# The last scan group of a Mamba-2 layer: ScalarE copies the gate units out of PSUM and applies the SiLU in place

## The reference

```
y = y + xs * d_skip
y = rmsnorm(y * silu(z), gnorm_w)
out = y @ w_out
```

## Time and profile before

| | |
|---|---|
| median of 3 runs | 1328.11 us (1326.69 to 1330.75) |
| the profiled execution, its own time | 1329.49 us |
| its span between first and last instruction | 1327.8 us |
| PE / DVE / ACT / POOL busy | 89% / 69% / 44% / 7% of the span |
| granted TensorE clock, mean | 0.949 of full |
| the last group, from its first x turn to the gated result | about 351 us to 432 us of the span |

### The profile page before, as it was taken

The page is one execution under the profiler, slowest core; times in us unless marked ns, Lnnn a source line. Parts: engine busy times, 40 slices in busy tenths (PEclk is TensorE's granted clock), DMA queues, the critical chain, the costliest instruction groups (busy, mean ns, idle before and its releaser), DMA issues.

```text
span 1327.8 us, 20149 instructions
## 1 busy us (share of the span) xinstructions
PE 1187.1 (89%) x7100; PEld 687.7 (52%) x7100; DVE 915.0 (69%) x1430; ACT 588.5 (44%) x1021; POOL 92.9 (7%) x106
## 2 busy tenths in 40 slices
PE   4999898998987689699999999997999968799997
PEld 2544464554544334244444444445845537688886
DVE  5696767758766889887888877637256656666554
ACT  4564654545545432233333432223334534566542
POOL 0004022050130000000000000000000000000000
PEclk9999898998999799799999999998999988899998
DMA  9331120111111446255645544430222102355552
GB/s 389 127 100 70 55 95 32 63 63 63 63 65 45 178 163 245 98 192 188 233 187 212 193 178 185 144 123 29 99 99 92 63 1 95 127 191 203 201 195 96
DMA packets 24526, 173.93 MB, mean 131 GB/s; under 512 B 2720, under 2 KB 2720, under 8 KB 5536
## 3 DMA queue, kind: packets, MB, share of 16 engines
q1 hardware_dynamic: 18432, 128.24, 26.2%
q0 software_dynamic: 5184, 37.75, 8.0%
q10 hardware_dynamic: 864, 7.34, 1.5%
HBM read 172.27 MB, written 1.05 MB: 131 GB/s over the span
## 4 chain that ended last, share of the span: by engine, by line
PE 73%; DVE 16%; issue 4%; ACT 4%; POOL 2%; DVEq 1%; DMA 0%; ACTq 0%; SPq 0%; POOLq 0%
PE bank L1482 19%; PE bank L1483 19%; PE bank L1484 19%; PE bank L1828 1%; DVE arena L995 1%; DVE arena L865 1%; PE bank L1686 1%; PE bank L1842 1%; PE bank L1675 1%; DVE arena L912 1%; PE bank L1509 1%; DVE wl L835 1%; DVE ssq L894 1%; DVE arena L907 1%; PE bank L1815 1%
## 5 line engine op out<-in xcount | busy, mean ns | idle before, releaser
L1482 PE MATMUL bank<-hh,wh 128*128 128x512 f16 (+1 forms) x1136 | 392.5, 346 | 20.6 <-DVE hl L903 7.7
L835 DVE SCALAR_TENSOR_TENSOR wl<-raw,wh 128x1024 f16<-128x1024 f32 x224 | 267.3, 1209 | 202.3 <-ACT wh L407 200.2
L1483 PE MATMUL bank<-hl,wh 128*128 128x512 f16 (+1 forms) x1136 | 391.8, 345 | 0.0
L1484 PE MATMUL bank<-hh,wl 128*128 128x512 f16 (+1 forms) x1136 | 391.4, 345 | 0.0
L407 ACT ACTIVATE wh<-raw 128x1024 f16<-128x1024 f32 x224 | 229.1, 1043 | 283.7 <-PE bank L1484 214.9
L1482 PE MATMUL bank<-arena,wh 128*128 128x512 f16 (+1 forms) x544 | 182.1, 335 | 11.1 <-DVE wl L835 3.7
L1483 PE MATMUL bank<-arena,wh 128*128 128x512 f16 (+1 forms) x544 | 182.0, 335 | 0.0
L1484 PE MATMUL bank<-arena,wl 128*128 128x512 f16 (+1 forms) x544 | 181.9, 334 | 0.0
L1482 PEld LDWEIGHTS bank<-hh,wh 128*128 128x128 f16 x1136 | 112.5, 99 | 123.9 <-issue 42.5
L865 DVE SCALAR_TENSOR_TENSOR arena<-arena,araw 128x1024 bf16<-128x1024 f32 x144 | 167.6, 1220 | 0.2
L1484 PEld LDWEIGHTS bank<-hh,wl 128*128 128x128 f16 x1136 | 112.4, 99 | 93.3 <-issue 5.7
(11 more groups left out here) (226 smaller groups left out, 1372.9 us busy)
## 6 DMA issues: line engine op xcount, KB each, us to landing
raw<-wgu SPq DMA_DIRECT2D x44, 1024.0 KB, 4.8
arena<-wadaT POOLq DMA_DIRECT2D x36, 1024.0 KB, 5.1
raw<-wdn SPq DMA_DIRECT2D x16, 896.0 KB, 4.5
raw<-wxg SPq DMA_DIRECT2D x12, 1024.0 KB, 4.9
arena<-wada SPq DMA_DIRECT2D x8, 1024.0 KB, 19.2
raw<-wz SPq DMA_DIRECT2D x8, 1024.0 KB, 4.8
raw<-wout SPq DMA_DIRECT2D x8, 1024.0 KB, 4.9
raw<-wdn SPq DMA_DIRECT2D x8, 1024.0 KB, 4.8
```

The lines of the kernel that those rows point to most:

```text
L835: ve.scalar_tensor_tensor(wl[:, u.slot, a:b], raw[:, u.slot, a:b], WS, wh[:, u.slot, a:b], ALU.mult, ALU.subtract).then_inc(lo_done, 1)
L1482: pe.matmul(o, wh[:, u.slot, wsl], ahi[:, k, t0:t1], start=st, stop=False)
L1483: pe.matmul(o, wh[:, u.slot, wsl], alo[:, k, t0:t1], start=False, stop=False)
L1484: i = pe.matmul(o, wl[:, u.slot, wsl], ahi[:, k, t0:t1], start=False, stop=en)
```

## The change

In the last group only, `z_raw` takes the place of `z_out`. It copies both banks into `zs` with Copy (counted by a new semaphore `zr_ok`) and then runs SiLU over `zs` in place, from SBUF to SBUF (counted by `zs_ok` as before). TensorE's waits ahead of units 1 and 2 go from `zs_ok` to `zr_ok`. The scale of 1/(WS*AS) moves to the copy.

```
+            def z_raw(k, u):
+                act.wait_ge(unit_done, u.half + (UD + 2))
+                for m in range(2):
+                    act.activation(zs[:, m, :], GB[m][:, :], ACT.Copy, scale=1.0 / (WS * AS)).then_inc(zr_ok, 1)
+                for m in range(2):
+                    act.wait_ge(zr_ok, 2 * k + m + 1)
+                    act.activation(zs[:, m, :], zs[:, m, :], ACT.Silu).then_inc(zs_ok, 1)
...
                 square_z(0)
-                z_out(u)
+                z_raw(0, u)
                 cvt(u.plus(2))
...
                 act.wait_ge(gl_ok, 2)
-                z_out(u.plus(1))
+                z_raw(1, u.plus(1))
                 square_z(2)
...
                 act.wait_ge(gl_ok, 4)
-                z_out(u.plus(2))
+                z_raw(2, u.plus(2))
...
+                    elif k == 0:
+                        pe.wait_ge(zs_ok, 2 * g + 1)
                     else:
-                        pe.wait_ge(zs_ok, 2 * g + 1 + 2 * k)
+                        pe.wait_ge(zr_ok, 2 * k)
```

More of the change, by code:

```diff
@@ L272, in build @@
         in_x = [sem("in_x0"), sem("in_x1")]
-        in_x_again, zp_ok = sem("in_x_again"), sem("zp_ok")
+        in_x_again, zp_ok, zr_ok = sem("in_x_again"), sem("zp_ok"), sem("zr_ok")
         in_ada = [sem(f"in_ada{i}") for i in range(ADA_FIRST)]
```

## The result

The changed kernel takes 1329.44 us (median of 20 runs, 1328.24 to 1330.80) against 1327.30 us for the kernel before (median of 20 runs, 1325.40 to 1330.75): 2.1 us more, a ratio of 1.0015 with a 95% interval of 1.0009 to 1.0022. It is slower, by less than the 0.3% named in the prediction.

What follows compares the result with a forecast made beforehand. ScalarE's path from unit 1's end to TensorE's `exponents` (3, 1) was taken as the bound. 0 (unit 0) + 1.2 (unit 1) + 0 (unit 2) + 1.7 (clock) = +2.9 us on 1328.11, so 1331.0 us; range 1327.3 to 1333.0.

Steps and rivals of the forecast that it cites:

- Unit 1, the first wait: TensorE's wait ahead of unit 2: copies without a table load let it start 1.29 us earlier.
- Unit 1, ScalarE's added time: ScalarE before `exps` (2, 3): two SBUF SiLUs at 0.52 each plus a 0.12 drain add 1.2 us.
- Where they meet: TensorE ahead of `exponents` (3, 1): the wait for `exps` (2, 3) grows from 1.30 to about 3.8 us, losing 1.2.
- Units 0 and 2: Last group's other two units: ScalarE's delay at unit 0 is covered, TensorE does not wait at unit 2; cost 0.
- the prediction's bound for unit 0: ScalarE at unit 0: if slower by 1.4 us, less 0.5 of cover, up to 0.9 us is lost.
- The clock: TensorE behind the 3.8 us pause: the clock falls to its lower level, costing 1.7 us (bounds 0 to 2.2).
- seven parts in ten: Chance given to TensorE losing its full clock behind the 3.8 us pause ahead of `exponents` (3, 1).
- The sum: Whole kernel: 0 for unit 0, 1.2 for unit 1, 0 for unit 2, 1.7 for the clock, +2.9 us.
- the rival in which the clock holds: TensorE behind the second pause keeps its clock; only ScalarE's 1.2 us is lost, 1329.3 us; chance 0.25.

Runs made afterwards that it cites:

- e4: Changed kernel with unit 1's two in-place SiLUs run twice: 1331.67 us against 1326.71 for the kernel before, ratio 1.0035.
- e5: Changed kernel with unit 1's SiLUs moved behind the group's last `exps` and VectorE's `gate(1)` moved later: 1325.25 us against 1328.75 for the kernel before.
- e2: Kernel before with the change at units 0 and 2 only, unit 1 keeping `z_out`: 1328.59 us against 1328.75 for the kernel before.
- a1: The changed kernel timed again, unaltered, on another chip: 1330.06 us against 1326.71 for the kernel before, ratio 1.0021.
- e1: Kernel before with the change at unit 1 only, units 0 and 2 keeping `z_out`: 1330.35 us against 1328.75 for the kernel before.
- e3: Changed kernel with TensorE writing step (3, 0)'s exponents eight times over, filling its second pause: 1329.69 us against 1328.75 for the kernel before.
- e6: The changed kernel with step (3, 0)'s exponents written eight times, timed again on another chip: 1328.67 us against 1326.71 for the kernel before.

## Why the prediction came out as it did

**Unit 1, the first wait.** Right: TensorE gained 1.43 us there (3.05 to 1.62), and none of it arrived at the end. The forecast was 1.29.

**Unit 1, ScalarE's added time.** Forecast 1.2 us, measured 1.05. The 0.12 for a drain ahead of the load is there, but I did not see that the copies, with no load ahead of them, begin 0.13 before `exps` has ended. The two cancel and leave the two SiLUs. The waits on `zr_ok` cost nothing that shows.

**Where they meet.** The second pause was forecast at 3.8 us and is 3.76. e4 lengthens ScalarE's list and the pause follows; e5 shortens it and the pause is gone. This shows that `exps` (2, 3), and not the emptying of the banks, sets this stretch.

**Units 0 and 2.** Costed at 0. e2 measures 0.01 us less on unit 0's ruler and 0.00 in the group. The slack was as thin as reckoned: `gate` waited 0.27 us for its SiLU. The Trainium skill (ScalarE: Activation LUTs, What ACT_TABLE_LOAD costs) adds a drain of 1.38 us to a table load. Here the trace does not agree: the copies end at 374.05, the load starts at 374.07 and ends at 375.35, and the SiLU starts at 375.36. No run here shows the drain. The 1.4 us in the prediction's bound for unit 0 stands in no row either; what the runs show there is `exps` (1, 0) 1.75 us late and nothing lost.

**The clock.** It fell, as forecast, in each of the four traces with this pause at 3.76 to 4.81 us (changed kernel, a1, e1, e4), and in neither of the two in which work filled it. The size was too small: 1.7 forecast, 2.14 measured on the path. I had reckoned `within` at its full-rate time and it too ran at half. So seven parts in ten looks too low for this pause, though all four traces are of longer executions (1330.45 to 1332.80 us) and none is from the lower heap. The sentence of the Trainium skill on idle gaps (TensorE: Matmul & The Clock Gate, Why this matters for your kernels; the prediction gives another section's name) was the better guide here, though the equal pauses of 3.05 in the earlier trace rows still part ways.

**The sum.** Forecast +2.9, the group in the trace +2.98, out of 1.05 + 2.14 - 0.23. That the two are so near is in part luck: ScalarE's term was 0.15 too high, the clock's 0.44 too low, and the -0.23 was not foreseen.

The time itself rose by 2.1 (1.2 to 2.9 by the interval), to 1329.44 where 1331.0 was forecast. Of these 1.6 us, 0.8 are the kernel before, whose median over 20 runs is 1327.30 and over the first three was 1328.11; the other 0.8 are the smaller rise. That 1329.44 lies next to the rival in which the clock holds (1329.3) does not speak for it: the traces show the clock fall, and the median lies between two heaps, of which the lower is 1.2 us above the kernel before, as that rival would have it, and the upper 2.8, as the forecast would.

In the profiled pair the rise is 1.1 us only, because of the clock elsewhere: 2.1 us at the end of attention that the kernel before loses there, as e2, e4 and e5 lose all or most of them, and the traces of the changed kernel, a1 and e1 do not. Whether that, or the lower heap, explains the medians is open. Why this stretch is slow in one program's trace and not in the other's was not tested.

## What to carry to other kernels

An engine that is released earlier gains nothing if its next wait is for the same engine that released it: look up the second wait, and count what the change adds ahead of it. Emptying PSUM early pays only if the work taken off (here the SiLUs and, with them, two table loads) goes behind what others wait for, and not right back in front of it: that is what lies between the change and e5, 6.6 us in the group. And when two idle times of the matmul engine are traded for each other, the longer one that results can cost the clock: here 2.14 us, twice the 1.05 us that ScalarE's added work cost.

## What the runs showed of the hardware

The clock can fall under work as well as under idle time. In the changed kernel it had fallen before TensorE's pause of 3.76 us was over (0.84 over the pause, 0.50 right behind it). And at the end of the group, TensorE runs 32 matmuls of 128x2 one behind the other (the adaLN projection, L1509 before). In the kernel before they took 4.39 us, though TensorE was busy all through: the granted clock was full for the first 2.5 us and then fell. In e3, e4, e5 and e6 they took 3.63. The rows, two stretches before and one in e5:

```profile
423.00:425.50 2.50, 2.50 (x25) 2.50 (x23) 0.00 (x0) 2.28 (x4) 0.00 (x0) 1.00 0.00 0
425.60:427.30 1.70, 1.70 (x9) 1.66 (x9) 0.00 (x0) 1.70 (x3) 0.00 (x0) 0.51 0.00 0
```

```profile
419.00:423.00 4.00, 3.71 (x34) 3.59 (x32) 1.31 (x4) 2.92 (x6) 0.00 (x0) 1.00 0.00 0
```

The matmuls are the same in both; what differs is when they start. Why the clock fell in the one and not in the other is not shown. This is the 0.76 us by which e3 undercuts the +1.06 of its ScalarE, and part of e5's gain.
